# A two-layer hybrid trunk on one core: the first attention four heads at a time, its buffers in the place of x, other orders for loads, rounds and retention

## What is computed

```python
for l in range(DEPTH):                                   # DEPTH = 2
    h = rmsnorm(x, norm_mix[l])
    proj = h @ w_in[l]
    (u, dq, dk, dv, iq, ik, iw, rq, rk, rv, rg) = jnp.split(proj, split_pts, axis=-1)
    y_a = s5_mixer(u, ...)                               # state space model, width 256
    y_b = dsa_attention(dq, dk, dv, iq, ik, iw, rel_bias)  # 8 heads of 64, one key and value head
    y_c = retention(rq, rk, rv, rg, ret_gn[l])           # 4 heads of 64, in chunks of 128
    x = x + concatenate([y_a, y_b, y_c]) @ w_out[l]
    h = rmsnorm(x, norm_ffn[l])
    gate, up = jnp.split(h @ w_ffn_in[l], 2, axis=-1)
    x = x + (jax.nn.silu(gate) * up) @ w_ffn_out[l]
return rmsnorm(x, norm_final)
```

## Time and profile before

| | |
|---|---|
| median of 3 runs | 2903.6 us (2901.05 to 2906.95) |
| the profiled execution | 2907.97 us |
| its span (first to last instruction) | 2905.5 us |
| PE busy | 2638.2 us |
| DVE busy | 1558.2 us |
| mean granted clock of PE | 0.947 |

### The profile page before, as it was taken

How to read it: one execution, slowest core, us unless ns; L and a number is a source line. 1 busy time by engine, 2 the same in 40 slices (tenths; PEclk the granted TensorE clock), 3 DMA queues, 4 the chain that set the end, 5 groups by cost and what they waited for, 6 DMA issues and landing times.

```text
span 2905.5 us, 34447 instructions
## 1 busy us (share of the span) xinstructions
PE 2638.2 (91%) x13482; PEld 2082.5 (72%) x13482; DVE 1558.2 (54%) x2784; ACT 1013.9 (35%) x1484; POOL 1313.1 (45%) x814
## 2 busy tenths in 40 slices
PE   7877787888999998899999999988899999999999
PEld 5656554576777776678877777757677777788887
DVE  3567822759899622673333147565989972211111
ACT  4222133333443443332334532333344344322222
POOL 3331122444544555354545452344454555555655
PEclk9978886999999999999999999989999999999999
DMA  6321110212222225222322242212222222433332
GB/s 154 86 87 40 37 30 8 73 51 68 75 81 69 73 73 156 70 83 75 87 75 87 59 125 75 66 51 59 66 74 79 70 71 76 162 95 97 105 117 88
DMA packets 389737, 230.25 MB, mean 79 GB/s; under 512 B 33577, under 2 KB 376521, under 8 KB 387529
## 3 DMA queue, kind: packets, MB, share of 16 engines
q1 hardware_dynamic: 388256, 225.44, 26.4%
q10 hardware_dynamic: 1320, 2.62, 0.5%
HBM read 211.78 MB, written 14.16 MB: 78 GB/s over the span
## 4 chain that ended last, share of the span: by engine, by line
PE 70%; DVE 18%; issue 3%; ACT 3%; POOL 3%; DMA 2%; SPq 0%; DVEq 0%; ACTq 0%; POOLq 0%
PE psum L1638 66%; DVE scores L1268 4%; DVE top L1266 4%; PE psum L1933 2%; POOL w_lo L646 2%; DMA w_raw<-in_w_in_dram 1%; DVE scores L1257 1%; DVE xs L1093 1%; DMA w_raw<-in_w_out_dram 1%; ACT scratch L971 1%; ACT w_hi L753 1%; POOL h_lo L654 1%; DVE psum L1299 0%; PE psum L1819 0%; DMA x_half<-xs 0%
## 5 line engine op out<-in xcount | busy, mean ns | idle before, releaser
L646 POOL TENSOR_TENSOR w_lo<-w_raw,w_hi 128x1024 fp32r<-128x1024 f32 (+2 forms) x408 | 899.5, 2205 | 1365.1 <-ACT w_hi L753 1345.5
L1638 PE MATMUL psum<-h_hi,w_hi 128*128 128x512 f32 x1984 | 807.4, 407 | 38.8 <-POOL w_lo L646 26.3
L1638 PE MATMUL psum<-h_hi,w_lo 128*128 128x512 f32 x1984 | 786.3, 396 | 0.0
L753 ACT ACTIVATE w_hi<-w_raw 128x1024 fp32r<-128x1024 f32 (+2 forms) x408 | 397.5, 975 | 1088.8 <-PE psum L1638 1003.5
L1638 PE MATMUL psum<-h_lo,w_hi 128*128 128x512 f32 x1984 | 772.0, 396 | 0.2 <-POOL h_lo L654 0.2
L1638 PEld LDWEIGHTS psum<-h_hi,w_hi 128*128 128x128 f32 x1984 | 383.0, 193 | 151.8 <-POOL w_lo L646 36.8
L1638 PEld LDWEIGHTS psum<-h_hi,w_lo 128*128 128x128 f32 x1984 | 381.4, 192 | 81.9
L1638 PEld LDWEIGHTS psum<-h_lo,w_hi 128*128 128x128 f32 x1984 | 380.4, 192 | 79.0 <-issue 2.1
L1266 DVE MAX8 top<-scores 128x8 f32<-128x512 f32 (+5 forms) x384 | 342.0, 891 | 7.8
L1268 DVE MATCH_REPLACE8 scores<-top,scores 128x512 f32<-128x512 f32 (+5 forms) x384 | 336.3, 876 | 0.0
L1638 PE MATMUL psum<-a_hi,w_hi 128*128 128x512 f32 x704 | 282.0, 401 | 6.8 <-DVE xs L1093 6.8
(11 more groups left out here) (284 smaller groups left out, 3032.0 us busy)
## 6 DMA issues: line engine op xcount, KB each, us to landing
w_raw<-in_w_ffn_in_dram SPq DMA_DIRECT2D x176, 512.0 KB, 3.8
w_raw<-in_w_ffn_out_dram SPq DMA_DIRECT2D x96, 384.0 KB, 3.5
w_raw<-in_w_in_dram SPq DMA_DIRECT2D x68, 512.0 KB, 3.8
w_raw<-in_w_out_dram SPq DMA_DIRECT2D x32, 512.0 KB, 4.2
w_raw<-in_w_ffn_out_dram SPq DMA_DIRECT2D x32, 256.0 KB, 2.7
x_half<-xs SPq DMA_DIRECT2D x6, 1024.0 KB, 6.5
xs<-x_half SPq DMA_DIRECT2D x6, 1024.0 KB, 8.0
out_dram<-mixed SPq DMA_DIRECT2D x8, 512.0 KB, 3.7
```

Source lines behind the costliest of these rows:

```text
L646: eng.tensor_tensor(w_lo(u, n), w_raw[:, u % 3, 0:n], w_hi[:, u % 2, 0:n].bitcast(F32), ALU.subtract).then_inc(sems["weights_ready"], 1)
L753: act(w_hi[:, u % 2, 0:n], w_raw[:, u % 3, 0:n], ACTF.Copy).then_inc(sems["hi_ready"], 1)
L1638: return eng.matmul(out_, lhsT, rhs, start=start, stop=stop, skip_group_check=True)
```

## The change

1. **First attention.** For (0, 0), `step_pairs` is 2: a step has four heads, in four PSUM banks C0, C1, D0, D1. The probabilities and their turned copies lie in `xs` (as `x_flat`), the four masks in `area`. x of half 0 is stored from `xs` (`store_x0`, two transfers of 1 MB) after the fillnorm of u18 and read back (`load_x0`) after the last block; the additions of mixout (0, 0) wait for it.
2. **Rounds and retention.** All 32 rounds of block 2 are in u8 to u14, before 20 there and 12 in u16 and u17. Retention steps 0 to 2 of (0, 0) come between u15 and u17, ahead of the second fillnorm. The rounds of block 3 stand half in u18 to u31, half among the blocks 0 to 2 of the attention (u32 to u36), before all in u18 to u31. `s5_set` is woven over u4 to u6.
3. **Planner's costs.** All side steps but rounds (as before) count 5.0, and a DMA step 1.0, so all are spaced differently: in the FFN of (0, 1) an attention step per unit at most, the three first score steps over two units.
4. **Loads.** The 18 parameter loads are single steps among the weights: for layer 0 in u0 to u3; for layer 1 ten of them in the FFN of (0, 0) (u88 to u106, one for two units), four in u126 and four from u128. The load of `xa` is four transfers at u125 and u126. The norm gains are loaded as rows of 512 bytes on ACT's queue, turned on PE and copied by DVE. Some waits for the constants come later.
5. **Bias table.** DRAM holds eight rows (12 KB, before 1536 KB); the skewed read goes the other way, and the masks on POOL read the windows backwards.

```diff
-    if step[0] == "attend":
-        return 0.3 + (1.7, 2.2)[step[5]] * NK[step[3]] / 1000
-    if step[0] == "scores":
-        return 2.0
-    if step[0] == "s5":
-        return 5.0
-    return 3.0
+    return 1.0 if step[0] == "dma" else 5.0
...
+def step_pairs(l, h):
+    return 2 if (l, h) == (0, 0) else 1
...
-    out += weave(main[:7], side)
+    out += weave(main[:4], blend(param_steps(0), side)) + weave(main[4:7], [("s5_set", 0, s) for s in range(5)])
-    out += weave(main[7:15], sc[:3] + blend(rounds(2, 0, 20), sc[3:]))
-    out += main[15:16] + [("rstd", "boot"), ("spread", "fill")] + weave(main[16:18], rounds(2, 20))
+    out += weave(main[7:15], sc[:3] + blend(rounds(2), sc[3:]))
+    out += main[15:16] + [("rstd", "boot"), ("spread", "fill")] + retention_steps(0, 0, 0, 2) + main[16:17]
+    out += retention_steps(0, 0, 2, 3) + main[17:18]
...
-    out += weave(main[:14], blend(retention_steps(0, 0) + s5, rounds(3)), 0)
-    side = [s for b in range(TT) for s in attend_steps(0, 0, b)] + [("attend_end", 0, 0, s) for s in range(2)]
-    out += weave(main[14:], side, 0, 12)
+    out += weave(main[:14], blend(retention_steps(0, 0, 3) + s5, rounds(3, 0, 16)), 0)
+    side = blend(att[0] + att[1] + att[2], rounds(3, 16)) + att[3] + [("attend_end", 0, 0, s) for s in range(2)]
+    out += weave(main[14:], side, 0, 6)
+    out += [("dma", "load_x0", 0)]
...
-    out += weave(main[1:N_OUT], [("rstd", None), ("spread", "fill"), ("dma", "params1", 0)], 0, 5)
+    side = [("rstd", None), ("spread", "fill")] + [("dma", "load_xa", n) for n in range(4)] + param_steps(1)[10:14]
+    out += weave(main[1:N_OUT], side)
...
-                where, n = (area, HALF) if (l, h) == (0, 0) else (scratch, T)
+                heads, n = (4, HALF) if self.first else (2, T)
+                where = x_flat if self.first else scratch
...
-        bias_dram = nc.dram_tensor("bias_rows", [HEADS, P, 384], F32).ap()
+        bias_dram = nc.dram_tensor("bias_rows", [HEADS, 384], F32).ap()
...
-                                if l == 0:
-                                    eng.wait_ge(sems["unit_done"], u)
-                                    eng.dma_start(xa, x_tiles(0, 0, KT)).then_inc(sems["xa_loaded"], 16)
...
+                elif step[:2] == ("dma", "store_x0"):
+                    eng.wait_ge(sems["norm_tmp"], KT)
+                    for g in range(2):
+                        store_group(g, 0)
+                elif step[:2] == ("dma", "load_x0"):
+                    eng.wait_ge(sems["mat_ready"], TT)
+                    for g in range(2):
+                        load_group(g, 0)
+                elif step[:2] == ("dma", "load_xa"):
+                    a = 2 * step[2]
+                    eng.dma_start(xa[:, a:a + 2, :], x_tiles(0, a, a + 2)).then_inc(sems["xa_loaded"], 16)
...
-                    eng.dma_start(bias_dram, brow.unsqueeze(1).broadcast_to([HEADS, P, 384])).then_inc(
-                        sems["bias_stored"], 16)
+                    eng.dma_start(bias_dram, brow).then_inc(sems["bias_stored"], 16)
```

More of the change, by code:

```diff
@@ L170, in mix_and_ffn @@
         got += ffn[:1] + scales() + weave(ffn[1:], side[n_mix:], 0, len(ffn) - 11)
+        if (l, h) == (0, 0):
+            for n, step in enumerate(param_steps(1)[:10]):
+                got.insert(got.index(ffn[45 + 2 * n]), step)
         return got
@@ L668, in masks @@
                 at_ = attention[l, h]
-                nk = NK[b]
+                nk, heads = NK[b], 2 * at_.pairs
                 far = nk - 256
                 if (l, h, b, j) == (0, 0, 0, 0):
+                    eng.wait_ge(sems["const_loaded"], 16)
                     eng.wait_ge(sems["bias_loaded"], 16)
+                    eng.wait_ge(sems["y_gated"], 1)
+                    for g in range(2):
+                        eng.wait_ge(sems[f"x_out{g}"], 16)
                 if b >= 2 and j == 0:
@@ L735, in _ @@
                         masks(l, h, b, 0)
-                    elif s == 1 and j + 1 < PAIRS:
-                        masks(l, h, b, j + 1)
+                    elif s == 1 and j + step_pairs(l, h) < PAIRS:
+                        masks(l, h, b, j + step_pairs(l, h))
         @block.scalar
@@ L1642, in take @@
                 for g in groups:
-                    for sem, n in kept.pop(g, ()):
-                        eng.wait_ge(sems[sem], n)
+                    first, n = GROUPS[g]
+                    for b in range(first, first + n):
+                        for sem, count in kept.pop(b, ()):
+                            eng.wait_ge(sems[sem], count)
             def leave(g, sem, n=1):
-                kept[g] = [(sem, st.add(sem, n))]
+                count = st.add(sem, n)
+                first, banks = GROUPS[g]
+                for b in range(first, first + banks):
+                    kept[b] = [(sem, count)]
             def unit(g, u, sem, last=False):
```

216 lines of the change are left out of this document (122 added, 94 removed).

## The result

The changed kernel takes 2811.0 us (median of 4 runs, 2809.7 to 2818.4), the kernel before 2905.2 us (median of 4). The ratio is 0.968, 95% interval 0.967 to 0.970: 94 us less, where 97 were forecast (2806.6 us). The total was right; most of its terms were not, and that the total came out within 5 us is luck: an error of 13 us in A and one of 22 us the other way in C cancelled, with smaller ones beside them. That is what the comparison by stages shows. A stage here ends where PE has ended a unit; the numbers are from the two profiled executions (spans 2905.5 and 2808.3 us).

The account below looks back on a forecast made before the run. PE's work was taken as the bound (busy 91% of the span), plus its idle time and the clock's cost. Terms summed to -97 us against 2907.97, giving 2811.0, then 2806.6 us for the median; 8 in 10 range 2768 to 2855.

Parts of the forecast that it names:

- A: Opening, 0 to 155.6 us: about -10 us from the smaller bias store and interleaved parameter loads, less exposed DVE work.
- C: First attention, 383.2 to 510.3 us: about -17 us, with about half of the waits for exponentials and copies gone.
- the 10.1 go, with most of the slow clock behind it: Opening: the smaller bias store removes PE's 10.1 us wait for w_lo; with parameter loads, together -12 to -17 us.
- B: 155.6 to 383.2 us: about -35 us, from 23 us less PE idle time and 12 us of the clock's 31.
- 26 us to be had, 5 taken: First attention: of the 26 us that the low clock costs there, only 5 counted as gained.
- D: Half 1 of each layer: about -8 us each, -16 in all, from shorter waits for scores and retention step 2.
- E: Around 1100 us: about -10 us, -8 from x's later load in four transfers, -2 from units between score steps.
- no w_lo wait over 2 us: Sign expected near 1060 us if the later, split load of x removes PE's long waits for w_lo.
- F: Attention (1,0), 1280 to 1700 us: about -9 us, all 8.7 us of waits for L971 gone.
- the rival in which waits come back: Rival, about 2840 us, chance 0.22: DVE's chain sets the pace from 155.6 to 383.2 us, so packed steps wait for each other.
- the one in which the clock comes back: Rival, about 2778 us, chance 0.13: 1.2 GHz hardly occurs between 146 and 440 us, gaining another 29 us.
- The sentence on retention steps 0 to 2: Moved between u15 and u17, these steps meet one w_lo each and again cost 2 us or so, through SBUF locking.

Follow-up runs that it names:

- bias_only: The kernel before with only the small bias store (eight rows to DRAM, windows read backwards): 2894.3 us, ratio 0.9968.
- rounds2_late: The changed kernel with 12 rounds of block 2 moved to u18 to u26 and 24 instead of 16 rounds of block 3 in the attention: 2796.6 us.
- rounds2_back: The changed kernel with 12 rounds of block 2 in u16 and u17 again and retention steps 0 to 2 after the second fillnorm: 2801.2 us.
- params_row: The changed kernel with the 18 parameter loads of layer 0 in a row ahead of the weights of u3, as before: 2809.8 us.
- s5_apart: The changed kernel with S5 step 6 moved behind unit 28, so a unit stands between steps 5 and 6: 2799.5 us, ratio 0.9644.
- rounds3_back: The changed kernel with all 32 rounds of block 3 in u18 to u31 again and none in the attention: 2822.3 us, ratio 0.9718.
- two_heads: The changed kernel with two heads at a time in the first attention again, all else as changed: 2848.8 us, ratio 0.9808.
- cost_old: The changed kernel with the planner's former costs for attend, scores and s5 steps (others 3.0, a DMA step 1.0): 2809.6 us, ratio 0.9673.
- apart_more: apart_late with s5_set steps 0 and 1 in u4 and u5 and the (0, 1) FFN's norm spread earlier, which makes that norm wrong: 2780.8 us.
- xa_only: The kernel before with layer 1's x loaded by four transfers at u125 and u126 instead of one of 2 MB before u123's weights: 2908.6 us.
- apart_late: rounds2_late with S5 steps 4, 5 and 6 of layer 0 in three places, one unit between each: 2789.9 us, ratio 0.9609.

## Why the prediction was right or wrong, step by step

**A was wrong: +4.6 us instead of -10, about +3 on equal work.** (The row that it reads as 15.3 us has 15.4.) The step that failed was "the 10.1 go, with most of the slow clock behind it". The wait went (bias_only), but DVE's chain of `s5_set` and scores stood 5 us behind it and became the wait; 7 of the 12 to 17 us were won in the stage, 9 to 10 by the medians. The second failure was the price of the crammed DVE work: I took 5 us of 25 as exposed, and u9 to u17 show 9.4. Some 3 of these are PE's work of retention step 2, which the prediction did not move; 12 rounds fewer give 4.6 back (rounds2_late). The third was not seen at all: the spacing of `s5_set` and the first scores costs 9 us in u4 to u8 against the kernels that spread the scores over three units (rounds2_back, rounds2_late). DVE was busy half of the stage, so the sum fitted; but its steps stood ahead of others for which PE waits. The 2 us for the parameter loads are nothing (params_row).

**B was right: -45 instead of -35, about -35 on equal work.** The 10 us between are the two steps that left the stage, which the prediction overlooked. The waits I named as going went: 11.7, 10.9 and 4.2 us. I gave only 7 of the 10.9, since I compared with one unit of cover; in fact the whole went. The idle time fell by 26.5 us where 23 were forecast. The clock's gain: 0.87 was forecast for u18 to u31 and 0.87 was measured; it gave 8 us where 12 were priced. The new wait for Z behind S5 step 5 is there as forecast: the sum for Z is 14.7 us where I had 10, and s5_apart shows that a unit between takes 7.8 of it away. But not all of the list caused the gain. rounds3_back shows that the rounds leaving the stage are worth 15 us, and rounds2_back that the move of the retention steps ahead of fillnorm was not needed to remove the 11.7.

**The clock in B.** PE's idle time in B fell from 57.3 to 30.8 us and the clock only rose from 0.82 to 0.87; in C the idle time was halved as well, and the clock rose from 0.73 to 0.96. The page "TensorE: Matmul & The Clock Gate" of the Trainium skill, section "HAM oscillation — how this bites in real kernels", puts a clock that falls again and again down to gaps in which PE waits for data. C agrees with it, and there it came nearer than my term. B neither agrees nor refutes it, since 30.8 us of gaps are left; the stretch at 0.66 with 1.3 us idle (last section) says that gaps are not all of it. Removing half of the gaps had two outcomes in two stages, so neither can be carried over alone.

**C was right in its waits and mis-sized in the clock: -32 instead of -17, about -39 on equal work.** The term that failed is "26 us to be had, 5 taken". I had -14 for waits; 27.8 became 11.7, -16. The clock rose from 0.73 to 0.96 and gave 24 us. two_heads confirms that it is the four heads: without them 46 us come back in u32 to u36, 19 of idle time and the rest clock. PE has no wait for weights or for x in the stage, so the cover for x's stores and loads held; and the rounds there are free (rounds3_back). Why the clock answers to four heads was not tried apart from the idle time.

**D failed in its sum.** In layer 0 the wait for the rotary products fell from 5.8 to 1.5 us and the scores from 13.8 to 10.3, as forecast, but u37 to u119 lost 0.2 us in all (0.3 to 4 in the experiments with the same steps there). Steps that moved by a unit met others: w_lo has two waits of 6.4 us in sum in u53 to u119 (1.0 before), the exponentials 12.3 instead of 9.5. u37 to u52 are 7 us shorter and u53 to u119 6.5 longer. cost_old, with the old spacing, takes 580.7 there, so the spacing is worth 2 to 6 us of the 8. The sentence "the rest of the moved steps lie in stages where PE is nearly always busy" named the reason why I did not look, and it was wrong: a stage with PE busy 93% of the time (u37 to u119) has steps that become waits when they are moved, too.

**E failed at the same place: -3 instead of -10.** The 6.5 us at u123 went (-7.8 for u120 to u127). At u136 the spread scores gave 8, and then u137 gave back 6 and u144, with the new wait of 6.8 us, 7; apart_more, which takes that wait away, wins only 3.4 of them, since the rounds then stand closer. The sign "no w_lo wait over 2 us" did not come either: one of 3.6 us stands in u128 to u135. That this part needs the parameter loads out of the way was only a half sentence in the prediction ("go elsewhere"); xa_only shows that without it the part costs 4 us instead of winning 7.

**F was right: -14 against -9**, with the waits for L971 (8.7 us) gone from the list. By cost_old the spacing is worth 9. The other 5 us are no more than what the stage varies by: kernels with the instructions of the one before take 512.1 to 517.4 us there.

**The sum.** Errors of +15 (A), -10 (B), -15 (C), +8 (D, layer 0), +7 (E) and -5 (F) add up to nothing; on equal work the first three are +13, 0 and -22. Layer 1's part of D was right at -7; cost_old has only 1 of it, so it goes with the spacing. The total lies in the range by luck: part of the rival in which waits come back happened in A, part of the one in which the clock comes back in C, and they cancelled. The terms B, C, D and E lay inside their own ends, A and F outside them.

**SBUF.** The sentence on retention steps 0 to 2 holds. DVE's and POOL's timelines of the changed kernel:

```profile
143.41 1.22 DVE L1367 TENSOR_TENSOR scratch<-scratch,cst 128x1024 f32<-128x1024 f32 x1
144.54 3.38 DVE L1368 TENSOR_TENSOR scratch<-scratch,cst 128x1024 f32<-128x1024 f32 x1
147.96 1.22 DVE L1370 TENSOR_TENSOR scratch<-scratch,cst 128x1024 f32<-128x1024 f32 x1
```

```profile
144.28 2.57 POOL L678 TENSOR_TENSOR w_lo<-w_raw,w_hi 128x1024 fp32r<-128x1024 f32 x1 [4.16 <-ACT w_hi L789]
```

L1368 takes 3.38 us beside w_lo, and L1367 and L1370 1.22 each: in its new place the step meets one w_lo, as in the earlier trace rows, and loses 2.2 us by it. "SBUF — State Buffer", section "SBUF: two separate sides", of the Trainium skill says that of a DVE operation with two inputs in SBUF and a GpSimd operation that reads SBUF the second waits for the whole of the first. The trace agrees: L1368 begins 0.26 us after w_lo and ends 1.1 us after w_lo's end at 146.85, close to the 1.22 us of one such multiplication.

## What to carry to other kernels

A wait that is taken away uncovers the next one on another engine; before pricing it in full, read when that engine's chain ends at the same place, and put only the distance between the two in the sum. Put a unit of other work between two steps of which the second waits for another engine's answer to the first (6 to 8 us less idle time of PE each here: s5_apart, apart_late), and put free work such as the rounds beside steps that leave its engine idle, not where its busy share merely has room. When one total is made of many moved steps, time the parts alone: here one part lost 3 to 10 us, two were worth nothing in sum, and one was worth something only with another. And before stages are compared, check that the same steps lie in them: two that crossed a border made A, B and C look other than they were.

## What the runs showed of the hardware that I had not expected

The clock can stay low while PE is hardly ever idle, and it does so in the same place in both kernels. Retention steps 5 and 6 and the unit behind them, before, after, and in params_row:

```profile
203.20:223.30 20.10, 18.78 (x91) 15.09 (x89) 6.61 (x17) 3.02 (x7) 2.35 (x1) 0.66 0.10 27
```

```profile
181.60:201.60 20.00, 18.67 (x90) 14.99 (x88) 5.17 (x14) 2.32 (x6) 2.35 (x1) 0.66 0.11 27
```

```profile
181.20:199.70 18.50, 17.18 (x90) 13.88 (x89) 5.16 (x14) 2.32 (x6) 2.35 (x1) 0.72 0.11 29
```

20.1 and 20.0 us, PE busy 18.8 and 18.7, clock 0.66 both times. In params_row, with the same instructions and the same 1.3 us of idle time, it is 18.5 us at 0.72: the clock of such a stretch is not fixed by its work either, which is where the 3 us between executions of u18 to u31 come from, at least in half. Against that u36 ran at 1.00 with PE idle for 10.4 of 45.0 us. What in the row of small products holds the clock down was not tried; idle time alone does not order these stretches.
